# Routing each tile of tokens while the output projection runs, in a decoder layer with 32 experts

## The chip, the cores and the metric

The kernel runs on one core of one Trainium2 chip. The metric is the device time of one execution in microseconds (us). Engines are named as in the profile: PE (TensorE), with PEld for its weight loads, DVE (VectorE), ACT (ScalarE), POOL (GpSimd) and SP (SyncE, which here only issues DMAs).

## What is computed

The reference is one layer on 1,024 tokens plus 16 meta tokens, width 1,024:

```
h = concat(meta_tokens, x)                       # 1040 x 1024
y = mlstm_mixer(h, ...)                          # chunked linear attention, ends with out @ w_out
h = layer_norm(ALPHA * h + y, ln1_g, ln1_b)
grp_logits = h @ w_group + b_group               # 4 groups
g_top = argmax(grp_logits)
exp_logits = (h @ w_router + b_router)           # 4 groups x 8 experts
top_vals, top_idx = top_k(exp_logits of group g_top, 2)
weights = softmax(grp_logits)[g_top] * softmax(top_vals)
for each expert e, on its tokens:  y += weight * (silu(x @ w_gate[e]) * (x @ w_up[e])) @ w_down[e]
h = layer_norm(ALPHA * h + y, ln2_g, ln2_b)
```

Each expert's gate, up and down matrices are 1,024 x 512, 1,024 x 512 and 512 x 1,024 numbers. Blocks of up to 128 tokens of one expert are called items here. There is one item for each of the 32 experts, and up to 16 more where an expert has over 128 tokens.

## The kernel before

All engines run their own instruction streams and meet at semaphores; the order on each engine is written out by hand. Large matrices are multiplied as three products: a tensor is split into a high part (`whi`, `xhi`, made by ACT) and a low part (`wlo`, `xlo`, the rest, made by DVE), and PE adds high x high, high x low and low x high (`mm3`, L1332 to L1334).

The stages are: input projections; eight chunks of attention (`scores`, `values`, `keys`, `attend`); the output projection, tile by tile (128 tokens each); the routing; the experts; the second layer norm.

**Output projection.** `out_half(i, q)` computes half of tile i's rows on PE (24 products of 128x512). On DVE `residual(i, q)` adds the scaled residual into `z1`, and `row_norm(i)` makes the normalised rows: `bn_stats` and `bn_aggr` for mean and variance, a subtraction and a product with `g1` (L1057), `rsqrt_column` (ten small operations), and a last pass (L1061) into `h1t`. POOL stores `h1t` to memory (`h1_rows`). PE transposes it (`h1_T`, L1555), ACT copies the transpose to `h1T`, and PE computes the 36 logits of the tile (`logits`, L1563); DVE adds the bias (L1066) into `lg`. On PE the order is `out_half(i, 0)`, `logits(i - 2)`, `out_half(i, 1)`, `h1_T(i - 1)`.

**Routing.** When the logits of all eight tiles are there, DVE works on all tiles at once: the best group, the best two of its eight experts, one-hot rows (`r_oh`), and their running sum over the tiles (`r_acum`). PE turns these into each token's rank in its expert's list (L1602 to L1604). DVE turns ranks into an item number and a slot, for the lists past 128 tokens as well (`r_kn`, `r_eq`, `r_ohr`, L1226), and PE adds up the token lists with 32 products (L1608). From them DVE makes `tokrow` (which row of `h1_rows` each slot of each item takes) and `dstrow`, and signals `routed`. SP, ACT and POOL wait for `routed`.

**Experts.** POOL copies the item's column of `tokrow` into `tix` and gathers the rows into `xg` with an indirect DMA (L537). PE transposes them (`rows_T`, L1619), ACT and DVE split them (`xg_hi`, `xg_lo`), and PE runs gate, up and down. `lo_expert(j, k, p)` on DVE (L1104) makes the low part of half p of matrix k of item j; `times_up` (L1262) multiplies the activated gate with up, `hidden_T` (L1649) transposes the product, and `hidden_lo` (L1266) splits it. The order on PE in `item(j)` is `up(j)`, first part of the gate of j+1, `hidden_T(j)`, the rest of that gate, `rows_T(j + 2)`, `down(j)`. Items 0 and 1 stand ahead of a loop, the last two behind it. SP loads a half matrix as soon as `lo_expert` has released its buffer.

Of the kernel before, what the change touches and what calls it, by code (L numbers as in the profile page):

```python
# [12 lines left out]
P = 128  # L13
# [32 lines left out]
COLS = (4, 5, 0, 1, 2, 3)  # L46

# [18 lines left out]
def build(nc, hcat, w_in, b_gates, head_norm_w, w_out, ln1_g, ln1_b, w_group, b_group, w_router,  # L66
# [7 lines left out]
    ys = nc.dram_tensor("expert_rows", (2 * T, D), F32).ap()  # L74

# [47 lines left out]
    lmv = at("lmv", [P, 4])  # L123
    lg = at("lg", [P, NT, GROUPS + NE])
# [49 lines left out]
    wgr = at("wgr", [P, KC, GROUPS + NE])  # L174
    bgr = at("bgr", [P, GROUPS + NE])
# [7 lines left out]
    ks = at("ks", [P, H, P])  # L183

# [25 lines left out]

    cursor[0] = route_base
    KN = 2 * NT
    r_iota = at("r_iota", [P, P])
    r_eq4 = at("r_eq4", [P, NT, GROUPS])
    r_oh4 = at("r_oh4", [P, NT, GROUPS])
    r_g4 = at("r_g4", [P, NT, GROUPS])
    r_prod = at("r_prod", [P, NT, GROUPS, PER_GROUP])
    r_in = at("r_in", [P, NT, PER_GROUP])
    r_t8 = at("r_t8", [P, NT, PER_GROUP])
    r_oh8 = at("r_oh8", [P, 2, NT, PER_GROUP])  # L220
    r_s = at("r_s", [P, 16, NT])
    r_kn = at("r_kn", [P, 10, KN])
    r_oh = at("r_oh", [P, KN, NE])
    r_pr = at("r_pr", [P, KN, NE])
    r_rk = at("r_rk", [P, NT, NE])
    r_cnt = at("r_cnt", [P, NE])
    r_ex8 = at("r_ex8", [P, NE, 8])
    r_ex = at("r_ex", [P, 4, NE])
    r_c8 = at("r_c8", [P, KN, 8])
    r_thr = at("r_thr", [P, 8])  # L230
    r_a = at("r_a", [P, NT + 1, NE], BF16)
    r_acum = at("r_acum", [P, NT + 1, NE], BF16)
    r_ohr = at("r_ohr", [P, KN, P], BF16)
    r_eq = at("r_eq", [P, KN, ITEMS], BF16)
    r_rhs = at("r_rhs", [P, 2, KN, ITEMS], BF16)
    r_val = at("r_val", [P, 2, KN])
    r_v = at("r_v", [P, 2, ITEMS])
    r_e = at("r_e", [1, 3, ITEMS])
    r_cmp = at("r_cmp", [1, EXTRA, NE])
    assert cursor[0] <= route_base + 2 * PIECE * 4  # L240
# [12 lines left out]
    Z_BANK = (0, 1, 4, 5)  # L253

    S = {}

    def sem(name):
# [24 lines left out]
        gtok_mm g_neg g_exp g_one g_ln g_lf b_mm g_a aT_mm m_rows mb_mm g_arg gate_exp  # L282
# [3 lines left out]
        r_exp r_arg r_hot r_item rk_mm r_rhs_done v2_mm routed pool_passed  # L286
# [34 lines left out]
    def _(sp):  # L321
# [71 lines left out]
        sp.dma_start(wgr[:, :, GROUPS:], w_router.rearrange("(p k) n -> p k n", k=KC)).then_inc(N["ln1_in"], 16)  # L393
        sp.dma_start(bgr[:, 0:GROUPS], vec(b_group, P)).then_inc(N["ln1_in"], 16)
        sp.dma_start(bgr[:, GROUPS:], vec(b_router, P)).then_inc(N["ln1_in"], 16)
# [5 lines left out]
        sp.dma_start(b1[:], vec(ln1_b, P)).then_inc(N["ln1_in"], 16)  # L401
        for c in range(2, NT):
            load_qk(c)
            load_o(c)
        sp.wait_ge(N["v_mm"], len(VU))
# [12 lines left out]
        sp.wait_ge(N["routed"], 1)  # L418
# [36 lines left out]
    def _(pool):  # L455
# [20 lines left out]
        g.memset(ones[:], 1.0).then_inc(N["consts"], 1)  # L476

# [16 lines left out]
        pool.wait_ge(N["lo_done"], lo_count(4))  # L494
        for b in range(2):
            last = g.memset(vext[b][:, :, DV:DV + 1], 1.0)
        last.then_inc(N["ones_ready"], 1)

        for i in range(NT):
            pool.wait_ge(N["h1_done"], i + 1)  # L500
            pool.dma_start(h1_dram[i * P:(i + 1) * P, :], h1t[i % 2][:]).then_inc(h1_stored[i % 2], 16)

        pool.wait_ge(N["y_mm"], 2 * NT)
        g.iota(r_iota[:].bitcast(I32), [[1, P]], base=0, channel_multiplier=0)
        g.iota(r_thr[:].bitcast(I32), [[P, 8]], base=P, channel_multiplier=0)
# [45 lines left out]
        for j in range(4):  # L551
            gather(j, j % 2)
# [1166 lines left out]
```

## Time and profile before

| | us |
|---|---|
| median of 3 runs (lowest, highest) | 1224.57 (1224.02, 1225.34) |
| the profiled execution | 1223.59 |
| its span in the profile | 1221.4 |
| PE busy | 1074.9 (88%) |
| DVE busy | 796.3 (65%) |
| ACT busy | 615.6 (50%) |

The span is what the profiler covers; what lies around it took 2.2 us in the profiled execution. A line of a timeline gives the start, the duration, engine, line, operation, output<-input by the names of the program, shape, count, and in square brackets how long the engine was idle before and which instruction ended that. The granted clock (PEclk) is a share of 2.4 GHz: 1.00 is 2.4 GHz and 0.50 is 1.2 GHz.

### The profile page before, as it was taken

To read this page: it belongs to the slowest core of one execution; us is meant where nothing else is said; L and a number is where in the kernel's file an instruction comes from. 1 tells how busy PE (TensorE), PEld (TensorE's weight loads), DVE (VectorE), ACT (ScalarE), POOL (GpSimd) and SP (SyncE) were. 2 spreads that over 40 slices of the span, in tenths; PEclk is the share of its full clock that TensorE was granted. 3 is DMA by queue.
4 is the path that set the end of the run, shared out by engine and by line. 5 is a ranking of instruction groups with operands and counts; after the bars stand their busy time and mean duration, and the time that the engine had idled before them with its cause. 6 is when DMAs were issued, how large, how long until landed. Compare 5 with 4: busy or idle time off the path is not lost.

```text
span 1221.4 us, 15159 instructions
## 1 busy us (share of the span) xinstructions
PE 1074.9 (88%) x5217; PEld 890.4 (73%) x5217; DVE 796.3 (65%) x1038; ACT 615.6 (50%) x655; POOL 219.5 (18%) x207
## 2 busy tenths in 40 slices
PE   6999999999999899813799999999999999999700
PEld 5878899588887688713688888888888888888500
DVE  3310421234646675563798889899888989988378
ACT  4311221123335210110878888887888888788511
POOL 2001111000000000013033323323332332232100
PEclk9999999999999899955899999999999999999955
DMA  7513314302013222332799999999999999998672
GB/s 247 186 70 121 112 44 124 108 18 69 36 69 104 104 87 86 115 144 87 278 366 360 387 389 382 389 404 378 377 388 380 376 384 394 387 384 314 244 305 103
DMA packets 62616, 284.00 MB, mean 233 GB/s; under 512 B 13896, under 2 KB 13896, under 8 KB 36976
## 3 DMA queue, kind: packets, MB, share of 16 engines
q1 hardware_dynamic: 49584, 254.09, 54.8%
q0 software_dynamic: 12992, 29.38, 6.5%
q8 instruction: 24, 0.39, 0.1%
q14 instruction: 16, 0.13, 0.0%
HBM read 266.61 MB, written 33.55 MB: 246 GB/s over the span
## 4 chain that ended last, share of the span: by engine, by line
PE 85%; DVE 7%; DMA 3%; issue 2%; DVEq 1%; ACT 1%; POOL 0%; SPq 0%; POOLq 0%
PE bank L1332 25%; PE bank L1333 24%; PE bank L1334 24%; PE bank L1619 2%; PE bank L1649 1%; PE bank L1514 1%; PE bank L1516 1%; PE bank L1519 1%; DMA raw_out<-l_w_out 1%; PE bank L1563 1%; DVE hh L1310 1%; DVE yy L1316 1%; DMA xt<-hcat 1%; DMA xg<-h_rows,tix 1%; PE bank L1476 1%
## 5 line engine op out<-in xcount | busy, mean ns | idle before, releaser
L1332 PE MATMUL bank<-whi,xghi 128*128 128x512 f32 x512 | 204.4, 399 | 2.8 <-DVE xglo L1257 1.4
L1334 PE MATMUL bank<-whi,xglo 128*128 128x512 f32 x512 | 201.1, 393 | 0.0
L1333 PE MATMUL bank<-wlo,xghi 128*128 128x512 f32 x512 | 200.7, 392 | 0.0
L1104 DVE TENSOR_TENSOR wlo<-raw_down,whi 128x2048 fp32r<-128x2048 f32 x64 | 146.5, 2292 | 37.0 <-ACT whi L727 37.0
L1332 PE MATMUL bank<-whi,xhi 128*128 128x512 f32 (+1 forms) x400 | 163.6, 409 | 2.7 <-ACT vext L664 1.6
L1333 PE MATMUL bank<-wlo,xhi 128*128 128x512 f32 (+1 forms) x400 | 159.2, 398 | 0.0
L1334 PE MATMUL bank<-whi,xlo 128*128 128x512 f32 (+1 forms) x400 | 158.5, 396 | 0.0
L1104 DVE TENSOR_TENSOR wlo<-raw,whi 128x2048 fp32r<-128x2048 f32 x64 | 146.3, 2288 | 8.2 <-ACT whi L727 7.2
L1104 DVE TENSOR_TENSOR wlo<-raw_up,whi 128x2048 fp32r<-128x2048 f32 x64 | 146.2, 2285 | 0.0
L727 ACT ACTIVATE whi<-raw_up 128x2048 fp32r<-128x2048 f32 x64 | 122.3, 1914 | 24.7 <-PE bank L1334 24.7
L727 ACT ACTIVATE whi<-raw_down 128x2048 fp32r<-128x2048 f32 x64 | 122.3, 1912 | 23.7 <-PE bank L1334 23.7
L547 POOL DMA_INDIRECT expert_rows<-yt,dix x32 | 58.6, 1830 | 380.9 <-ACT yt L750 380.9
L727 ACT ACTIVATE whi<-raw 128x2048 fp32r<-128x2048 f32 x64 | 122.2, 1913 | 2.5 <-PE bank L1334 0.9
L1332 PEld LDWEIGHTS bank<-whi,xghi 128*128 128x128 f32 x512 | 97.5, 190 | 22.8 <-DVE xglo L1257 1.8
L1334 PEld LDWEIGHTS bank<-whi,xglo 128*128 128x128 f32 x512 | 97.0, 189 | 20.9
L1333 PEld LDWEIGHTS bank<-wlo,xghi 128*128 128x128 f32 x512 | 97.3, 190 | 19.2
L1332 PE MATMUL bank<-whi,ghi 128*128 128x512 f32 x256 | 102.2, 399 | 1.4 <-DVE glo L1266 1.4
L1334 PE MATMUL bank<-whi,glo 128*128 128x512 f32 x256 | 100.2, 391 | 0.0
L1333 PE MATMUL bank<-wlo,ghi 128*128 128x512 f32 x256 | 100.1, 391 | 0.0
L1332 PEld LDWEIGHTS bank<-whi,xhi 128*128 128x128 f32 (+1 forms) x400 | 75.0, 188 | 22.2 <-issue 3.1
L1334 PEld LDWEIGHTS bank<-whi,xlo 128*128 128x128 f32 (+1 forms) x400 | 74.6, 187 | 19.6
L1333 PEld LDWEIGHTS bank<-wlo,xhi 128*128 128x128 f32 (+1 forms) x400 | 74.8, 187 | 16.4
(298 smaller groups left out, 1590.8 us busy)
## 6 DMA issues: line engine op xcount, KB each, us to landing
raw<-l_w_gate SPq DMA_DIRECT2D x64, 1024.0 KB, 7.8
raw_up<-l_w_up SPq DMA_DIRECT2D x64, 1024.0 KB, 7.9
raw_down<-l_w_down SPq DMA_DIRECT2D x64, 1024.0 KB, 8.3
raw<-l_w_in SPq DMA_DIRECT2D x5, 2048.0 KB, 9.8
yy<-expert_rows SPq DMA_DIRECT2D x8, 1024.0 KB, 12.2
xt<-hcat SPq DMA_DIRECT2D x8, 512.0 KB, 3.3
o_rows<-stage POOLq DMA_DIRECT2D x16, 256.0 KB, 2.6
qkT<-qk_rows SPq DMA_DIRECT2D x16, 256.0 KB, 3.5
```

Of the source, the lines that this page charges most:

```text
L547: g.indirect_dma_start(ys[0:2 * T, :], bass.IndirectOffsetOnAxis(dix[b][:].bitcast(U32), 0), yt[b][:], None, bounds_check=last_row, oob_is ...
L727: a.activation(whi[k][:, halves(p)], raw_e[k][:, halves(p)], ACT.Copy).then_inc(e_hi[k], 1)
L1104: tt(wlo[k][:, halves(p)], raw_e[k][:, halves(p)], whi[k][:, halves(p)].bitcast(F32), ALU.subtract).then_inc(e_lo[k], 1)
L1310: stt(hh[n], yy[n][:, 1, :], wts[:, n, 1:2], hh[n], ALU.mult, ALU.add, accum_out=fsum[:, n:n + 1])
L1316: stt(yy[n][:, 1, :], hh[n], fneg[:, n:n + 1], g2, ALU.add, ALU.mult)
L1332: t.matmul(out, lh, rh, start=first, stop=False)
L1333: t.matmul(out, lh, rl, start=False, stop=False)
L1334: return t.matmul(out, ll, rh, start=False, stop=last)
L1476: last = t.matmul(ps[F_BANK[1]][:, h * P:(h + 1) * P], qkT[b][:, 1, h, :], qkT[b][:, 0, h, :], start=True, stop=True)
L1514: t.matmul(ps[N_BANK[h % 2]][:, 0:DV + 1], ew[:, h, :], vext[c % 2][:, h, :], start=True, stop=False)
L1516: t.matmul(ps[N_BANK[h % 2]][:, 0:DV + 1], qsT[:, h, :], cst[:, h, :], start=False, stop=True).then_inc(N["n_mm"], 1)
L1619: last = t.transpose(ps[q][:, k * P:(k + 1) * P], xv[:, 4 * q + k, :], ident[:])
```

## The change

Routing is taken apart into a piece for each tile that runs during the output projection.

- The logits are computed from the rows before normalisation. With z the row, m its mean, r the reciprocal deviation, the logits are r * (z @ (g W) - m * (g @ W)) + b @ W + bias. So W is scaled by `ln1_g` on ACT once, the two rows g @ W and b @ W (`logit_constants`, 8 products on PE in the attention of chunk 2) go through memory to all partitions (`cgb`), and PE transposes `z1` (`z_T`) where it transposed `h1t`. The 4 group logits are padded to 8 columns.
- `top_two(i)` on DVE picks the group and the two experts of one tile with `max` and `max_index`, which give the eight largest values and their places. `ranks(i)` on PE and `slots(i)` on DVE give the rank in the list, and `token_list(i)` adds the tile's part to the lists in one PSUM bank, which collects over all eight tiles. Only slots 0 to 127 of each expert are handled there.
- `item_count` (how many items there are) comes after `routed` and has a semaphore of its own, `routed_n`. The lists past 128 tokens (`past_128`, `list_past_128`, `rows_past_128`) are made inside items 0 and 1, the expert weights (`expert_weights`, with two exponentials on ACT) in the last item.
- The rows are normalised and stored by `h1_rows(i)`, later than before in DVE's order; ACT issues the store (`h1_store`), where POOL did.
- The constants (`r_iota` and others) are made by POOL at the start of the kernel. The clearing of `xg` is gone, and the first six gathers take their index from `tokrow` with no copy.

`past_128` is 11 DVE operations, the last a one-hot of 128x2048 as `r_ohr` was (L1226); `list_past_128` is 32 products of 128x16 on PE.

The old routing of all tiles at once (L1127 to L1250, some 70 DVE operations) goes; it is not shown. The core of the diff ("..." marks what is left out):

```diff
 @block.scalar
+        def logit_constants():
+            act.wait_ge(N["cc_mm"], 1)
+            a.activation(ccs[:], ps[N_BANK[0]][0:2, CC_COLS], ACT.Copy).then_inc(N["cc_cp"], 1)
+            for k in range(KC):
+                last = a.activation(wgr[:, k, :], wgr[:, k, :], ACT.Copy, scale=gbc[:, k, 0:1])
+            last.then_inc(N["wg_scaled"], 1)
+            act.wait_ge(N["cc_cp"], 1)
+            act.dma_start(cc_dram, ccs[:]).then_inc(N["cc_out"], 16)
...
         for i in range(NT - 1):
-            h1_T(i)
+            z_T(i)
+            h1_store(i)
         act.wait_ge(N["y_mm"], 2 * NT - 1)
         for p in range(2):
             hi_expert(0, 0, p)
-        h1_T(NT - 1)
...
+        z_T(NT - 1)
+        h1_store(NT - 1)
         for p in range(2):
             hi_expert(0, 1, p)
-        act.wait_ge(N["routed"], 1)
...
 @block.vector
+        def stats(i):
...
+            rsqrt_column(lmv[:, b, 2:3], lmv[:, b, 1:2], lmv[:, b, 3:4])
+        def h1_rows(i):
...
+            stt(h1t[b][:], z1[b][:], lmv[:, b, 0:1], g1[:], ALU.subtract, ALU.mult)
+            dve.drain()
+            stt(h1t[b][:], h1t[b][:], lmv[:, b, 2:3], b1[:], ALU.mult, ALU.add).then_inc(N["h1_done"], 1)
...
+        def top_two(i):
+            b, row = i % 2, lg[:, i, :]
+            dve.wait_ge(N["lg_mm"], i + 1)
+            stt(row, cgb[:, 0, :], lmv[:, b, 0:1], ps[F_BANK[0]][:, 0:NL], ALU.mult, ALU.add).then_inc(N["lg_done"], 1)
+            dve.drain()
+            stt(row, row, lmv[:, b, 2:3], cgb[:, 1, :], ALU.mult, ALU.add)
+            dve.drain()
+            v.max(r_gv[:, i, :], row[:, 0:GPAD])
+            dve.drain()
+            v.max_index(r_gi[:, i, :], r_gv[:, i, :], row[:, 0:GPAD])
+            dve.drain()
+            tt(r_pen[:], iota_g, r_gi[:, i, 0:1].to_broadcast([P, GROUPS]), ALU.not_equal)
+            dve.drain()
+            stt(r_in[:].rearrange("p (g e) -> p g e", g=GROUPS), r_pen[:].unsqueeze(2).to_broadcast([P, GROUPS, PER_GROUP]), NEG,
+                row[:, GPAD:].rearrange("p (g e) -> p g e", g=GROUPS), ALU.mult, ALU.add)
+            dve.drain()
+            v.max(r_tv[:, i, :], r_in[:])
+            dve.drain()
+            v.max_index(r_ti[:, i, :], r_tv[:, i, :], r_in[:])
+            dve.drain()
+            tt(r_oh[:, i], iota_e, r_ti[:, i, 0:2].unsqueeze(2).to_broadcast([P, 2, NE]), ALU.is_equal)
+            dve.drain()
+            tt(r_a[:, i, :], r_oh[:, i, 0, :], r_oh[:, i, 1, :], ALU.add).then_inc(N["r_hot"], 1)
+            wait(dve, N["list_mm"], i - 1)
+            tt(r_rhs[b][:, 0], r_oh[:, i], r_val0[:].unsqueeze(2).to_broadcast([P, 2, NE]), ALU.mult)
+            ts(r_rhs[b][:, 1], r_oh[:, i], float(2 * P * i), None, ALU.mult)
+            dve.drain()
+            tt(r_acum[:, i + 1, :], r_acum[:, i, :], r_a[:, i, :], ALU.add)
+        def slots(i):
+            dve.wait_ge(N["rk_mm"], i + 1)
+            dve.drain()
+            for k in range(2):
+                stt(r_junk[:, k, :], r_oh[:, i, k, :], 1.0, ps[F_BANK[0]][:, RANK_COLS], ALU.mult, ALU.mult, accum_out=r_rank[:, i, k:k + 1])
+            dve.drain()
+            tt(r_ohr[i % 2][:], iota_s, r_rank[:, i, :].unsqueeze(2).to_broadcast([P, 2, P]), ALU.is_equal).then_inc(N["r_slot"], 1)
...
+        for i in range(3, NT):
             residual(i, 0)
-            if i > 1:
-                logits(i - 2)
+            top_two(i - 1)
+            h1_rows(i - 1)
+            slots(i - 1)
             residual(i, 1)
-            row_norm(i)
+            stats(i)
+        top_two(NT - 1)
...
+        h1_rows(NT - 1)
+        slots(NT - 1)
+        dve.wait_ge(N["list_mm"], NT)
+        token_rows(F_BANK[1], LIST_COLS, 0).then_inc(N["routed"], 1)
         for p in range(2):
             lo_expert(0, 0, p)
...
+        item_count()
+        xg_lo(0, 0)
         for p in range(2):
             lo_expert(0, 1, p)
-        xg_lo(0, 0)
         xg_lo(1, 1)
...
         def item(j, b, ahead=2):
...
             hidden_lo(j)
+            if not ahead:
+                expert_weights()
+            if isinstance(j, int) and j == 1:
+                rows_past_128()
...
                 lo_expert(j + 1, 2, 0)
                 lo_expert(j + 1, 2, 1)
+            if isinstance(j, int) and j == 0:
+                past_128()
 @block.tensor
         out_half(1, 0)
         out_half(1, 1)
         gated_T(NT - 1)
-        out_half(2, 0)
-        h1_T(0)
-        out_half(2, 1)
+        out_half(2, 0, range(0, 2))
+        z_T(0)
+        out_half(2, 0, range(2, KC))
         logits(0)
-        h1_T(1)
+        z_T(1)
+        out_half(2, 1, range(0, 4))
+        ranks(0)
+        out_half(2, 1, range(4, KC))
+        token_list(0)
+        logits(1)
         for i in range(3, NT):
-            out_half(i, 0)
-            logits(i - 2)
-            out_half(i, 1)
-            h1_T(i - 1)
-        logits(NT - 2)
-        h1_T(NT - 1)
+            out_half(i, 0, range(0, 2))
+            z_T(i - 1)
+            if i == 3:
+                ranks(1)
+            out_half(i, 0, range(2, KC))
+            if i == 3:
+                token_list(1)
+            logits(i - 1)
+            out_half(i, 1, range(0, 4))
+            ranks(i - 1)
+            out_half(i, 1, range(4, KC))
+            token_list(i - 1)
+        z_T(NT - 1)
         logits(NT - 1)
+        ranks(NT - 1)
+        token_list(NT - 1)
...
         def item(j, b, ahead=2):
...
             hidden_T(j)
+            if isinstance(j, int) and j == 1:
+                list_past_128()
```

## Rows read from the trace of the kernel before

**Rows 1.** The page: busy time, share and instructions of each engine.

```profile
PE 1074.9 (88%) x5217; PEld 890.4 (73%) x5217; DVE 796.3 (65%) x1038; ACT 615.6 (50%) x655; POOL 219.5 (18%) x207
```

**Rows 2.** Waits: engine, line, releaser: us in total, times, longest us.

```profile
PE bank L1602 <- DVE r_acum L1172: 14.9, 1, 14.9
PE bank L1608 <- DVE r_rhs L1228: 12.3, 1, 12.3
PE bank L1649 <- DVE gu L1262: 5.7, 2, 4.8
...
DVE hh L1307 <- DMA yy<-expert_rows: 16.6, 2, 15.4
```

**Rows 3.** The chain that ended last, in order of time: start, us, what.

```profile
483.92 0.89 PE bank L1555 x8
...
504.19 1.71 PE bank L1563 x16
...
559.28 9.30 DMA xg<-h_rows,tix
...
572.07 0.79 PE bank L1332
```

**Rows 4.** Timeline of DVE in the output projection.

```profile
483.96 0.69 DVE L1044 SCALAR_TENSOR_TENSOR z<-hres,bank 128x512 f32<-128x512 f32 x1 [5.44 <-PE bank L1334]
484.74 1.29 DVE L1050 BATCH_NORM_STATS2 lst<-z 128x6 f32<-128x512 f32 x2
...
486.39 1.29 DVE L1057 SCALAR_TENSOR_TENSOR z<-z,lmv,g 128x1024 f32<-128x1024 f32 x1
...
490.02 1.29 DVE L1061 SCALAR_TENSOR_TENSOR h1t<-z,lmv,b 128x1024 f32<-128x1024 f32 x1
...
497.76 0.69 DVE L1044 SCALAR_TENSOR_TENSOR z<-hres,bank 128x512 f32<-128x512 f32 x1 [5.44 <-PE bank L1334]
...
511.57 0.69 DVE L1044 SCALAR_TENSOR_TENSOR z<-hres,bank 128x512 f32<-128x512 f32 x1 [5.12 <-PE bank L1334]
```

**Rows 5.** Timeline of DVE in the routing.

```profile
531.65 0.19 DVE L1136 TENSOR_TENSOR r_oh<-r_iota,r_s 128x32 f32<-128x32 f32 x1
531.91 0.43 DVE L1139 TENSOR_TENSOR r_prod<-lg,r_oh 128x256 f32<-128x256 f32 x1
532.41 0.29 DVE L1142 TENSOR_TENSOR r_prod<-r_prod 128x128 f32<-128x128 f32 x1
...
548.62 2.28 DVE L1226 TENSOR_TENSOR r_ohr<-r_iota,r_kn 128x2048 bf16<-128x2048 f32 x1
```

**Rows 6.** Timeline of ACT behind the output projection.

```profile
512.01 1.09 ACT L717 ACTIVATE h1T<-bank 128x512 f32<-128x512 f32 x2 [12.72 <-PE bank L1555]
512.99 3.71 ACT L727 ACTIVATE whi<-raw 128x2048 fp32r<-128x2048 f32 x2
```

**Rows 7.** DMA issues by line: KB each, median us to landing.

```profile
h_rows<-h1t POOLq DMA_DIRECT2D x8, 512.0 KB, 2.9
```

**Rows 8.** The gathered rows' tile, all 32 gathers.

```profile
DMA to landing us min/median/max: 4.1/9.0/10.4
```

**Rows 9.** Timeline of SP around the first gather.

```profile
558.50 2.53 SPq L382 DMA_DIRECT2D raw_up<-l_w_up  x2
```

**Rows 10.** Windows: busy us (instructions) by engine, PEclk, DMA share, GB/s.

```profile
592.00:593.00 1.00, 0.00 (x0) 0.00 (x0) 1.00 (x1) 1.00 (x1) 0.00 (x0) 0.87 0.95 336
...
599.00:600.00 1.00, 1.00 (x4) 0.74 (x4) 1.00 (x2) 0.00 (x0) 0.00 (x0) 0.72 1.05 442
```

**Rows 11.** Timeline of PE, the transposes in items 0 and 1.

```profile
594.35 1.13 PE L1649 MATMUL bank<-ident,gu 128*128 128x128 f32 x4 [4.83 <-DVE gu L1262]
614.56 0.63 PE L1649 MATMUL bank<-ident,gu 128*128 128x128 f32 x4
```

**Rows 12.** Timeline of DVE in item 1.

```profile
607.92 4.58 DVE L1104 TENSOR_TENSOR wlo<-raw_down,whi 128x2048 fp32r<-128x2048 f32 x2 [1.07 <-ACT whi L727]
612.78 0.69 DVE L1262 TENSOR_TENSOR gu<-sg,bank 128x512 f32<-128x512 f32 x1 [0.28 <-PE bank L1334]
```

More of the change, by code:

```diff
@@ new lines, in build @@
+    r_in = at("r_in", [P, NE])
+    r_ex = at("r_ex", [P, 3, NE])
+    assert cursor[0] <= offsets["hnw"]
+    r_rhsx = [over("r_oh", f"r_rhsx{i}", [P, 2, NT, 2, EXTRA], BF16)[:, i] for i in range(2)]
+    cursor[0] = offsets["qsT"]
+    r_ohr = [at(f"r_ohr{i}", [P, 2, P], BF16) for i in range(2)]
+    r_rhs = [at(f"r_rhs{i}", [P, 2, 2, NE], BF16) for i in range(2)]
+    r_junk = at("r_junk", [P, 2, NE])
+    r_t1 = at("r_t1", [P, NE])
+    r_big = at("r_big", [P, NE])
+    r_g4 = at("r_g4", [P, NT, GROUPS])
@@ L548, in scatter @@
                                  bounds_check=last_row, oob_is_err=False).then_inc(scattered[b], 16)
+        pool.wait_ge(N["routed"], 1)
+        for s in range(2):
+            pool.wait_ge(h1_stored[s], 16 * (NT // 2))
         for j in range(4):
@@ L704, in _ @@
                 gated_hi(c - 1)
+            if c == 2:
+                logit_constants()
             if c < NT - 1:
@@ L709, in _, with h1_store, z_T @@
         gated_hi(NT - 1)
-        def h1_T(i):
+        def h1_store(i):
+            act.wait_ge(N["h1_done"], i + 1)
+            act.dma_start(h1_dram[i * P:(i + 1) * P, :], h1t[i % 2][:]).then_inc(h1_stored[i % 2], 16)
+        def z_T(i):
             for q in range(2):
@@ L1091, in _ @@
         gate_rows(NT - 1)
-        row_norm(0)
+        stats(0)
         gated_lo(NT - 1)
-        for i in range(1, NT):
+        logit_terms()
+        residual(1, 0)
+        h1_rows(0)
+        residual(1, 1)
+        stats(1)
+        residual(2, 0)
+        top_two(0)
+        h1_rows(1)
+        slots(0)
+        residual(2, 1)
+        top_two(1)
+        stats(2)
+        slots(1)
+        for i in range(3, NT):
             residual(i, 0)
-            if i > 1:
-                logits(i - 2)
+            top_two(i - 1)
+            h1_rows(i - 1)
+            slots(i - 1)
             residual(i, 1)
-            row_norm(i)
-        logits(NT - 2)
+            stats(i)
+        top_two(NT - 1)
         def lo_expert(j, k, p):
@@ L1415, in maxima, with logit_constants @@
             last.then_inc(N["mb_mm"], 1)
+        def logit_constants():
+            pe.wait_ge(N["ln1_in"], 16 * 8)
+            pe.wait_ge(N["ones_ready"], 1)
+            pe.wait_ge(N["num_done"], 8)
+            for k in range(KC):
+                last = t.matmul(ps[N_BANK[0]][0:2, CC_COLS], gbc[:, k, :], wgr[:, k, :], start=k == 0, stop=k == KC - 1)
+            last.then_inc(N["cc_mm"], 1)
         pe.wait_ge(N["consts"], 1)
```

449 lines of the change are left out of this document (214 added, 235 removed).

## The prediction

> **What bounds the kernel now.** I read the page first: PE is busy for 88% of the span [rows 1], so a change pays where PE stands still, and costs wherever it makes PE wait. The list of waits comes next. PE waits 14.9 us for the running sum of one-hot rows and 12.3 us for the last list operand [rows 2]. Both belong to one stretch, which the chain in order of time and DVE's timeline show: the last product of the output projection ends at about 511.4 (DVE's residual starts at 511.57), the first gather is issued at 559.28, and the first expert product starts at 572.07 [rows 3, 4]. From 511.4 to 572.07, 60.7 us, PE does almost nothing, and the chain runs through DVE and one DMA. The change works on the first 47.9 us of it.
>
> The output projection ahead of it is bound by PE. DVE's residual starts at 483.96 and at 497.76 and waited 5.44 us for PE each time [rows 4]: a tile takes 13.80 us. Eight transposes take 0.89 and the logits 1.71 [rows 3], which leaves 11.20 for 48 products, 0.233 each. DVE's idle 5.44 us per tile are the only room for routing.
>
> **The per-tile pieces on DVE.** Two consecutive starts are the price of one step with its wait: 0.26 us for 32 elements (531.65 to 531.91) and 0.50 for 256 (531.91 to 532.41) [rows 5]. `top_two` up to `r_hot` is ten steps. Eight plain ones make 2.1 with the PSUM operand. The trace has no `max` or `max_index`. Bounds: `max_index` costs at least one plain step, 0.26, which makes 2.6 for the chain with small extras for pointer scalars; at most, eight separate passes over 32 elements, so one step of 256, 0.50 for each of the two `max` and the two `max_index`, and the chain is 3.75. I take 0.43 for `max_index` and 0.26 for `max`, nearer to the plain step because the rows are short: **2.95**. The rest of `top_two` is three steps, 0.60. `h1_rows` is two passes of 1.28 or 1.29 [rows 4], 2.65 with waits. `slots` is two steps of 32 and one of 256, 1.05. 
>
> **What that does to PE.** I count from the end of `out_half(i, 0)`, from tile 4 on. Logits ready +1.83; `r_hot` +4.78; end of `top_two` +5.38; `h1_rows` +8.03; `slots` +9.08. PE arrives at `ranks(i - 1)` at +4.5 and waits 0.3; it arrives at `token_list(i - 1)` at +7.9 and waits until +9.15, another 1.2. Then 0.3 for the list, 1.4 for six products, 0.95 for `z_T`, 4.2 for 18 products: the next round begins at **+16.0, not +13.8**. What queues behind these waits on PE is the output projection itself. Worked out in the same way, tiles 2 and 3 wait more, 8.1 us in all: `z_T(0)` comes earlier than `h1_T(0)` did and stands behind DVE's low part of the last attention rows (1.6), and `stats` stands in front of the first pieces. Tiles 4 to 7 wait 5.0. More PE work ahead of the last half tile: one more `z_T` and logits (2.6), seven `ranks` and six lists at 0.3 (3.9). Sum 8.1 + 5.0 + 6.5: the projection ends **19.5 us later**, at 530.8. The bounds of `top_two` give 17.0 and 25.
>
> The waits rest on a count of steps. The Trainium skill, VectorE: DVE Perf Modes, section on the TRN2 errata, says that each instruction pays a fixed latency, and that many small tiles pay it per tile. The trace agrees: 8 times the elements cost 0.50 against 0.26 [rows 5]. By this rule the per-tile form speaks against the change, since eight tiles pay 17 steps each for what one batch did in some 70.
>
> **The tail.** From 530.8: `residual(7, 1)` waits for `slots(6)` and ends at 532.6, `z_T(7)` at 533.7. ACT comes out of the store of tile 6 at 531.5 and must do the expert halves first, 3.7 [rows 6]; the copies (1.1) end at 536.3. The logits take between 1.71 and twice that, as the clock may fall in this pause; I take 2.5: 538.9. Then DVE: 2.95 + 0.6 + 2.65 make 545.2, `slots` 546.2, list 0.5, `token_rows` 0.85: `routed` at 547.6. POOL also waits for the store of tile 7, issued at 545.2 and landed after 2.9 [rows 7], 548.2; so this store is late last, not the lists. The gather goes out at **548.4**, 17.6 us after the projection where it was 47.9: **-30.3**.
>
> **The gather.** It took 9.3 us with two half matrices issued at 558.50 in front of it [rows 3, 9]; the quickest of 32 took 4.1 [rows 8]. Now `lo_expert(0, 0, 0)` ends at 549.9, and the halves that it releases are issued behind the gather. I take 7.0, between the two: **-2.3** (0 to -5.2). The 3.5 us from landing to the first product stay; DVE is out of `item_count` (about 4 us) at 556, in time.
>
> **Added work behind it.** `logit_constants` on PE: eight products like the logits, **+1.7** (0.8 to 3: ACT then has nine short operations and a DMA ahead of its copy of the values). `past_128` on DVE: the one-hot 2.28 [rows 5], two of 512 at 0.7, three of 256 at 0.43, two of 128 at 0.27, three short ones 0.6: 6.1 us. It stands straight in front of `times_up(1)`, which before waited 0.28 for PE after DVE's last low part (607.92 + 4.58) [rows 12]. So gate times up is ready at 619.3, and `hidden_T(1)`, which ran at 614.56 [rows 11], waits 4.8. In the equal pause of item 0 (4.83) the clock fell to 1.2 GHz in 592 to 593 and came back in 599 to 600, 5.2 us after PE resumed at 594.35 [rows 10, 11]; half of that, 2.5, is lost. `list_past_128`: 32 short products, 0.9. Sum **+8.2**. `expert_weights` costs DVE nothing, since DVE waits 15.4 us for the last rows [rows 2]; its exponentials delay ACT's last copies a little, **+0.4** (0 to 2).
>
> At nothing: the constants on POOL's queue at the start (it then waits for the first store anyway), SP's four small loads, ACT's issue of the stores. The cover is idle queue time; without it each costs under 1 us. `item_count` delays nothing, for `lo_expert(1, 0, 0)` waits for the activated gate.
>
> **Sum.** 19.5 - 30.3 - 2.3 + 1.7 + 8.2 + 0.4 = -2.8. The profiled execution has a span of 1221.4 and took 1223.59; it would be 1218.6 and 1220.8. It lies 1.0 under the median 1224.57, so the median is **1221.7**.
>
> **Rivals.**
> 1. *DVE's routing chain is longer than I count.* Each 0.1 us more in `top_two` comes eight times, seven tiles on PE and once in the tail: 0.8. At the upper bound, 3.75, this is +6.4: **1228**. It decides from 0.36 us per tile on. For it: four operations without a row, on a chain that is already what PE waits for. Against it: short rows, and all other short steps here cost the same. Chance 0.27.
> 2. *The clock falls in the projection too.* PE pauses 1.2 us per tile and in tiles 2 and 3 up to 1.7. If five of these cost 2.5 us like the one in item 0: **1234**. Against it: in item 0 the clock held for 3 us of pause before it fell [rows 10]. Chance 0.06.
> 3. *`past_128` is hidden*, because other work on DVE leaves room or PE's gate begins later: without stall and clock loss, -7.3: **1214**. Against it: the slack before `times_up(1)` was 0.28. Chance 0.15.
> 4. *The projection keeps its pace* (13.8 plus 0.6 a tile), and the change saves all that the waits promise: 13.1 less, **1209**. It needs DVE's chain shorter by some 1.5 us per tile. Chance 0.07.
>
> The forecast itself holds 0.45, with a range of its own of 1217 to 1226.
>
> **Numbers.** About 0.2% (2.4 us) can be told from no change in this kernel: under 1222.1 is faster, over 1227.0 slower. The forecast's case gives 0.24 faster, 0.14 same, 0.07 slower; rivals 3 and 4 give 0.22 faster; rival 1 0.05 same and 0.22 slower; rival 2 0.06 slower. So faster 0.46, same 0.19, slower 0.35. The range reaches from rival 3, with the gather at its quickest, 1212, to rival 2, 1234.
>
> **What would show it.** In the profile after: 16 us between residuals in the projection, PE waiting for DVE's `r_ohr` or `r_a` there; the last `out_half` ending near 532 (with `logit_constants` counted); the gather near 550, and the first expert product near 561; PE waiting 4.8 us for `gu` in item 1 and a second dip of the clock behind it. The forecast is wrong if `max_index` takes over 0.6 us, if the waits in the projection are small, or if the wait in item 1 is missing.

## The result and the profile after

The changed kernel takes 1217.31 us (median of 4 runs, 1216.20 to 1217.95), the kernel before, run beside it, 1224.95 us (4 runs, 1224.02 to 1225.77). The ratio is 0.9937, with a 95% interval of 0.9920 to 0.9954: 7.6 us or 0.6% faster. The profiled execution took 1216.2 us, with a span of 1213.5 where it was 1221.4.

The page gives the busy time of each engine, as in [rows 1]:

```profile
PE 1080.5 (89%) x5279; PEld 891.8 (73%) x5279; DVE 809.8 (67%) x1152; ACT 618.9 (51%) x665; POOL 206.5 (17%) x192
```

PE is busy 5.6 us longer than before, in a span that is 7.9 us shorter: it stands still less. The list of waits shows where:

```profile
PE bank L1731 <- DVE gu L1297: 10.0, 3, 4.8
PE bank L1629 <- DVE r_ohr L1150: 9.7, 8, 3.7
PE bank L1701 <- DMA xg<-h_rows,tokrow: 9.4, 1, 9.4
...
PE bank L1622 <- DVE r_a L1137: 4.7, 3, 2.9
PE bank L1615 <- ACT h1T L751: 2.5, 1, 2.5
PE bank L1607 <- DVE xlo L1066: 1.6, 1, 1.6
```

The two long waits of [rows 2], 14.9 and 12.3 us, are gone. In their place stand eight for `r_ohr`, 0.84 to 0.95 us each in the projection and 3.70 at the last tile, and three for `r_a`. The wait for `gu`, two times before, now comes three times. PE's timeline, with the wait ahead of each instruction in brackets:

```profile
497.57 0.26 PE L1629 MATMUL bank<-r_rhs,r_ohr 128*128 128x32 bf16 x4 [0.85 <-DVE r_ohr L1150]
512.99 0.27 PE L1629 MATMUL bank<-r_rhs,r_ohr 128*128 128x32 bf16 x4 [0.84 <-DVE r_ohr L1150]
528.40 0.27 PE L1629 MATMUL bank<-r_rhs,r_ohr 128*128 128x32 bf16 x4 [0.84 <-DVE r_ohr L1150]
529.00 1.16 PE L1607 MATMUL bank<-ident,z 128*128 128x128 f32 x8 [0.33 <-DVE z L1080]
532.65 3.64 PE L1615 MATMUL bank<-wgr,h1T 128*128 128x40 f32 x16 [2.50 <-ACT h1T L751]
539.23 0.21 PE L1622 MATMUL bank<-r_a,beforeb 128*128 128x32 bf16 x1 [2.94 <-DVE r_a L1137]
543.17 0.29 PE L1629 MATMUL bank<-r_rhs,r_ohr 128*128 128x32 bf16 x4 [3.70 <-DVE r_ohr L1150]
...
552.87 1.95 PE L1701 MATMUL bank<-ident,xg 128*128 128x128 f32 x8 [9.39 <-DMA xg<-h_rows,tokrow]
...
579.24 1.13 PE L1731 MATMUL bank<-ident,gu 128*128 128x128 f32 x4 [4.79 <-DVE gu L1297]
...
604.29 1.13 PE L1731 MATMUL bank<-ident,gu 128*128 128x128 f32 x4 [4.32 <-DVE gu L1297]
```

From one `r_ohr` to that of the next tile is 15.4 us, and each time PE waits 0.84 or 0.85 for it; behind the last product all waits are DVE's, ACT's and the gather's. The last line is the new stall in item 1, where PE waited for nothing in [rows 11]. Following the same points through both traces (starts in us; the forecast in the last column is the prediction's own sum) gives:

| point | before | after | shift | forecast |
|---|---|---|---|---|
| last product of the projection | 511.13 | 527.17 | +16.0 | +21.2 |
| first gather issued | 559.28 | 545.81 | -13.5 | -9.1 |
| first expert product | 572.07 | 556.23 | -15.8 | -11.4 |
| transposes of `gu` in item 0 | 594.35 | 579.24 | -15.1 | |
| transposes of `gu` in item 1 | 614.56 | 604.29 | -10.3 | |
| end of the span | 1221.4 | 1213.5 | -7.9 | -2.8 |

So 15.8 us are won up to the first expert product, and 7.9 are given back: 5.5 of it by the transposes of item 1, the rest by `gu` of item 2 (DVE starts it at 623.04, where it was 630.48: -7.4).

### The profile page after: what moved, and what is told of

Read it like the earlier page. It is cut to its first block, busy times and chain, and to the rows that moved or that the text cites. A ratio compares the mean times of both kernels' runs of the same rounds, so it can differ in the third digit from the quotient of the medians.

```text
span 1213.5 us, 15480 instructions
## 1 busy us (share of the span) xinstructions
PE 1080.5 (89%) x5279; PEld 891.8 (73%) x5279; DVE 809.8 (67%) x1152; ACT 618.9 (51%) x665; POOL 206.5 (17%) x192
## 4 chain that ended last, share of the span: by engine, by line
PE 81%; DVE 10%; DVEq 3%; DMA 2%; issue 2%; ACT 1%; SPq 0%; ACTq 0%; POOLq 0%
PE bank L1374 23%; PE bank L1376 23%; PE bank L1375 23%; PE bank L1701 2%; PE bank L1731 1%; PE bank L1615 1%; PE bank L1566 1%; PE bank L1568 1%; DVE wlo L1278 1%; PE bank L1571 1%; DMA xt<-hcat 1%; DVE h1t L1097 1%; DVE hh L1352 1%; DVE yy L1358 1%; DVEq L1096 1%
## 5 line engine op out<-in xcount | busy, mean ns | idle before, releaser
L1278 DVE TENSOR_TENSOR wlo<-raw,whi 128x2048 fp32r<-128x2048 f32 x64 | 146.4, 2289 | 10.3 <-ACT whi L761 9.0
L761 ACT ACTIVATE whi<-raw 128x2048 fp32r<-128x2048 f32 x64 | 122.4, 1915 | 15.8 <-PE bank L1376 14.1
L1375 PEld LDWEIGHTS bank<-wlo,xghi 128*128 128x128 f32 x512 | 97.8, 191 | 19.6
```

What stands on the lines that cost most here:

```text
L761: a.activation(whi[k][:, halves(p)], raw_e[k][:, halves(p)], ACT.Copy).then_inc(e_hi[k], 1)
L1278: tt(wlo[k][:, halves(p)], raw_e[k][:, halves(p)], whi[k][:, halves(p)].bitcast(F32), ALU.subtract).then_inc(e_lo[k], 1)
L1375: t.matmul(out, lh, rl, start=False, stop=False)
```

## Experiments

All kernels ran beside the kernel before, and ratios are to that. Differences in us are between medians. The kernel before had a median of 1224.95 us beside the changed kernel, 1225.18 beside experiments 1, 2 and 4, 1224.58 beside 3, 5, `h1_first` and `combined`, and 1223.49 beside `store_clear`, `count_first`, `combined_swap` and `best`; so a difference across these groups holds up to 1.7 us that no edit made, and there the ratios are the better guide. The runs also differ by some 3 us in where they stand when the projection's tail begins (`z_T(0)` starts between 430.4 and 433.7 in the profiles), so stretches are compared from starts inside one trace.

### 1. Top-8 operations done twice

```diff
 def top_two(i):
...
-    v.max(r_gv[:, i, :], row[:, 0:GPAD])
-    dve.drain()
-    v.max_index(r_gi[:, i, :], r_gv[:, i, :], row[:, 0:GPAD])
-    dve.drain()
+    for _ in range(2):
+        v.max(r_gv[:, i, :], row[:, 0:GPAD])
+        dve.drain()
+        v.max_index(r_gi[:, i, :], r_gv[:, i, :], row[:, 0:GPAD])
+        dve.drain()
...
```

The pair for `r_tv` and `r_ti` is doubled in the same way.

```diff
+    for _ in range(2):
+        v.max(r_tv[:, i, :], r_in[:])
+        dve.drain()
+        v.max_index(r_ti[:, i, :], r_tv[:, i, :], r_in[:])
+        dve.drain()
```

> Each pair of max and max_index in top_two is done twice, with the same results. By the starts in the changed kernel's timeline a pair is 0.56 and 0.60 us, so top_two is 1.16 us longer. Theory (the serial chain on DVE paces PE in seven tiles and the tail): 8 x 1.16 = 9.3 us more, 1226.6, period 16.6 us. Rival (PE's order absorbs part of it, since ranks waited for nothing from tile 3 on): less than 5 us more. A third outcome, the longer pauses lower the clock in the projection: over 13 us more.

Measured: 1226.38 us (1.0014, 1.0004 to 1.0025), 9.1 more than the changed kernel. The list of waits of this kernel:

```profile
PE bank L1624 <- DVE r_a L1139: 15.1, 8, 4.1
PE bank L1631 <- DVE r_ohr L1152: 9.2, 7, 3.7
```

The 0.5 us less for `r_ohr` and 10.4 more for `r_a` are what was added: PE now waits at `ranks` of every tile. DVE's residual starts at 503.71 and at 520.29, a period of 16.58 for 15.42 in the same order of the changed kernel. This is the prediction's slope, 0.8 us of time for each 0.1 us in `top_two`, found at 0.78. The granted clock stayed at 1.00 from 470 to 536; before that, behind a wait of 2.68 us at the first `ranks`, it was at 0.50 or on its way there or back from 444 to 448.

### 2. `slots` before `h1_rows`

```diff
 for i in range(3, NT):
     residual(i, 0)
     top_two(i - 1)
-    h1_rows(i - 1)
     slots(i - 1)
+    h1_rows(i - 1)
```

> In the loop of the projection (tiles 2 to 6) slots(i - 1) stands before h1_rows(i - 1) on DVE instead of behind it. Theory (the projection is slow because PE waits at each token list for r_ohr, behind the 2.65 us of h1_rows): the waits of 0.84 us at L1629 vanish, the period goes from 15.4 to 14.5 us, the time falls by 4.5 us to 1212.8. Rival (DVE's total work per tile sets the period, not the order): the wait moves to z_T or ranks, the period stays at 15.4, within 1 us of the changed kernel.

Measured: 1213.17 us (0.9906, 0.9887 to 0.9924), 4.1 less. Its list of waits:

```profile
PE bank L1629 <- DVE r_ohr L1150: 4.8, 3, 3.7
PE bank L1607 <- DVE xlo L1066: 1.6, 1, 1.6
PE bank L1607 <- DVE z L1080: 1.3, 1, 1.3
```

Five of the eight waits are gone, the period is 14.53 (residuals at 495.15 and 509.68), and DVE still waits 1.5 us per tile for PE. DVE's work per tile is the same, so these 0.9 us per tile came from its order: `r_ohr`, for which PE waits, stood behind the two passes of `h1_rows`. What remains over 13.80 is 0.7 a tile, in which PE waits for nothing from tile 4 on; `ranks` and the lists are what it has to do there beyond before.

### 3. The kernel before, with only the constants moved

```diff
 def _(pool):
...
+    g.iota(r_iota[:].bitcast(I32), [[1, P]], base=0, channel_multiplier=0)
...
+    g.tensor_copy(r_val[:, 1, :], r_val[:, 1, :].bitcast(I32)).then_inc(N["r_arg"], 1)
     for u in range(UNITS):
         store(u)
...
-    pool.wait_ge(N["y_mm"], 2 * NT)
-    g.iota(r_iota[:].bitcast(I32), [[1, P]], base=0, channel_multiplier=0)
...
-    g.tensor_copy(r_val[:, 1, :], r_kn[:, 1, :].bitcast(I32)).then_inc(N["r_arg"], 1)
```

> The kernel before, with only this of the change: POOL makes r_iota, r_thr and the token values at the start, in tiles of their own, instead of behind the projection. DVE waited 5.00 us for them at 530.48. Theory (those 5 us were on the path to the first gather): 5 us below the kernel before, 1219.9, so that over half of the measured 7.6 us could be had without routing by tiles. Rival (POOL's part runs beside, and something else, such as the last stores or the list operands, takes its place): under 1.5 us.

Measured: 1219.12 us (0.9950, 0.9935 to 0.9965), 5.5 less than the kernel before. In the timeline of the kernel before, POOL stood 9.28 us between making its integers and casting them, without a cause named by the profile, and DVE waited for it:

```profile
529.56 0.29 POOL L511 CAST r_iota<-r_iota 128x128 f32<-128x128 int32 x1 [9.28 <-issue]
...
530.48 0.19 DVE L1120 TENSOR_REDUCE r_s<-lg 128x8 f32<-128x32 f32 x1 [5.00 <-POOL r_val L515]
```

What POOL waited for at this drain is not shown. Its store of tile 7 was issued at 519.21 and took 8.4 us to land, to 527.6, so it was under way for most of that time. Without the wait the first reduction follows the last logits at once (524.30 and 524.60) and the token rows come 4.9 us sooner against the residuals. So 5.5 of the 7.6 us could be had with the routing left in one batch. Routing by tiles has them too, since it makes these constants at the start; over this kernel its own net gain is 1.8 us between medians. That is not clear of noise: the intervals of the two ratios, 0.9920 to 0.9954 and 0.9935 to 0.9965, overlap.

### 4. `past_128` moved, and left out

```diff
     for p in range(2):
         lo_expert(0, 1, p)
+    past_128()
     xg_lo(1, 1)
...
-        if isinstance(j, int) and j == 0:
-            past_128()
```

> past_128 moves on DVE from the end of item 0 to between lo_expert(0, 1) and xg_lo(1, 1), where DVE stood idle for 4.9 us. Theory (its 5.9 us stood in front of times_up(1), so that PE waited 4.3 us in item 1, the clock fell, and 8.4 us were given back): PE's second wait for gu is under 0.5 us, the dip of the clock in item 1 is gone, and the time is 7.5 us below the changed kernel, 1209.8. Rival (the 8.4 us come from list_past_128's 32 products or from the gathers' transfers, and DVE's block is not their cause): within 1.5 us of the changed kernel, 1216 to 1218, the wait for gu still there.

> Leaves out the lists of tokens past 128 per expert altogether: past_128 and its token rows on DVE, the 32 products on PE, and POOL's wait for them. Theory (DVE's block costs about 7.5 us, the 32 products 0.9): 8.4 us below the changed kernel, 1208.9, and 0.9 below the kernel with past_128 moved. Rival (part of what was given back behind the first gather is something else, such as transfers): the gap is under 6 us.

The second kernel has no `past_128`, no `list_past_128` and no `rows_past_128`, so it handles no token past the 128th of an expert. Measured: moved 1210.71 us (0.9882, 0.9864 to 0.9900), 6.6 less; left out 1209.10 us (0.9873, 0.9853 to 0.9893), 8.2 less. In the changed kernel DVE's timeline in item 1 reads:

```profile
593.18 4.58 DVE L1278 TENSOR_TENSOR wlo<-raw_down,whi 128x2048 fp32r<-128x2048 f32 x2 [1.07 <-ACT whi L761]
597.67 0.28 DVE L1191 TENSOR_TENSOR r_c<-r_rank,r_thr 128x128 f32<-128x128 f32 x1
...
601.35 2.29 DVE L1207 TENSOR_TENSOR r_ohrx<-r_iota,r_kn 128x2048 bf16<-128x2048 f32 x1
603.55 0.68 DVE L1297 TENSOR_TENSOR gu<-sg,bank 128x512 f32<-128x512 f32 x1
```

The `gu` of [rows 12] used to follow the low parts; now 5.9 us stand between them. And PE's timeline of the kernel with `past_128` moved:

```profile
582.11 1.13 PE L1730 MATMUL bank<-ident,gu 128*128 128x128 f32 x4 [4.79 <-DVE gu L1297]
...
602.74 0.63 PE L1730 MATMUL bank<-ident,gu 128*128 128x128 f32 x4
603.21 0.96 PE L1638 MATMUL bank<-r_rhsx,r_ohrx 128*128 128x16 bf16 x32
```

The pause in item 1 is gone and the transposes take 0.63 again, as in [rows 11], not 1.13. From the first expert product to `gu` of item 2 it is 66.8 us in the changed kernel, 60.4 with the block moved and 58.4 without it; the kernel before has 58.4. So what was given back is the handling of the lists past 128: 6.4 us by the place of `past_128`, 2.0 by the 32 products and what else remains. The rival (the gathers' transfers) is out.

### 5. ACT's copies first

```diff
+z_T(NT - 1)
 for p in range(2):
     hi_expert(0, 0, p)
-z_T(NT - 1)
 h1_store(NT - 1)
```

> ACT copies h1T of tile 7 before it does the two halves of whi (3.7 us). Theory (those halves stood in front of the copies, as the prediction says, so logits(7) came late and at half the clock): copies start near 529.9 instead of 531.5, PE's pause before logits(7) shrinks from 2.50 to about 0.7 us, top_two(7) starts as stats(7) ends, 3.3 us sooner, and the time falls by 3 us to 1214.3. Rival (the halves are needed as early as they are, so lo_expert(0, 0) and the first product move later by as much): within 1 us.

Measured: 1212.19 us (0.9899, 0.9884 to 0.9914), 5.1 less. PE's pause shrank to 0.78 as expected, and `top_two(7)` began 1.7 us sooner against the last residual, not 3.3, because the logits kept to half the clock (414 ns for each of 16, in both kernels) in spite of the shorter pause. The profiles give 1.7 us up to the first product and 1.2 by item 2, besides a `z_T(0)` that lay 0.9 earlier from causes ahead of the edit. What the 1.2 us behind the first product are is open; the direction and most of the expected 3 us are shown, the 5.1 of the medians (4.7 by the ratios) is more than the profiles account for.

### 6. The last tile: the store and the gather

```diff
+h1_rows(NT - 1)
 top_two(NT - 1)
...
-h1_rows(NT - 1)
 slots(NT - 1)
```

> For the last tile h1_rows(7) stands before top_two(7) on DVE, in the 3.36 us in which DVE waited for logits(7). Theory (from the last product to the gather DVE's own sequence is the path): routed comes 2.65 us sooner and the store of tile 7, which was last, is early; the gather goes out about 3.8 us sooner, near 542, and the time falls by 3.6 us to 1213.7. Rival (the first gather is held by something else, or the gain is lost to a colder clock or to SP's halves in front of the gather): under 1.5 us.

Measured: 1216.37 us (0.9929, 0.9917 to 0.9941), only 0.9 less: the expectation failed. The token rows were 2.4 us sooner (541.62 for 544.03), but the first product was 1.5 us later. Two lines of its timeline (POOL, SP), and one of its DMA issues between 530 and 560 (the last number is the us to landing), show why:

```profile
544.00 3.16 POOL L551 DMA_INDIRECT xg<-h_rows,tokrow  x1 [329.83 <-DMA h_rows<-h1t]
...
544.03 2.53 SPq L404 DMA_DIRECT2D raw<-l_w_gate  x2
```

```profile
h_rows<-h1t ACTq DMA_DIRECT2D x1, 512.0 KB, 6.8
```

The store of tile 7, issued at 536.24, fell among the loads of `raw_up` and `raw_down` and landed only at 543.0; and the gather left together with the halves of gate(1). The windows of 541 to 542 us, of h1_first and then of the changed kernel, show it: the DMA engines (second number from the end) are full in the first and idle in the second, just ahead of its own store at 542.24.

```profile
541.00:542.00 1.00, 0.08 (x4) 0.00 (x0) 0.76 (x4) 0.00 (x0) 0.00 (x0) 0.50 1.01 418
541.00:542.00 1.00, 0.00 (x0) 0.00 (x0) 1.00 (x1) 0.00 (x0) 0.00 (x0) 0.50 0.00 0
```

Two kernels took these apart, both with `h1_first` in them:

```diff
 # store_clear, SP
+sp.wait_ge(N["h1_done"], NT)
 load_expert(0, 0, 2)
 # count_first, DVE
+item_count()
 for p in range(2):
     lo_expert(0, 0, p)
-item_count()
```

> h1_first, and SP waits until h1_rows(7) has been made before it issues the halves of raw_down(0). In h1_first the store of tile 7 was issued 6.0 us sooner than in the changed kernel but took 6.8 us to land instead of 2.6, under the loads of raw_up and raw_down, and the gather went out 0.96 us behind its landing, 2.4 us behind the token rows. Theory (the store of tile 7 holds the gather, and the loads hold the store): the store lands in under 4.5 us, the gather goes out near 542.8 instead of 544.0, and the time is 1 to 2 us below h1_first. Rival (POOL needs 2 us from the token rows whatever the store does): the gather stays 2.4 us behind the token rows.

> h1_first, and item_count stands on DVE before lo_expert(0, 0) instead of behind it, so the half matrices of gate(1), which lo_expert releases, go out about 4 us later. In h1_first they were issued 0.03 us behind the gather, whose issue then took 3.16 us instead of 1.3 to 1.6, and PE got the rows 10.4 us behind the gather instead of 7.1. Theory (the collision with these loads costs the 3.3 us): PE gets the rows 5 to 7 us behind the gather, first product near 553.5, the time 3.5 to 4.5 us below h1_first, 1212.5. Rival (the gather is slow for another reason): 10 us and no gain.

Measured: store_clear 1216.21 us (0.9935, 0.9915 to 0.9955), no gain; count_first 1209.28 us (0.9869, 0.9845 to 0.9893), 7.1 less than h1_first, where 3.5 to 4.5 were expected. Its first product starts at 552.64 for 557.71, 5.1 sooner, and `gu` of item 2 is 6.4 sooner (617.74 for 624.12); where the last 1.3 of these arise is open. The wait on SP did not do what it was for: SP issued the loads at 536.37, in front of the store at 536.38, which again took 6.9 us. That run does not test the store against loads. It does show that the store holds the gather, together with the others (us; landing is issue plus the time to landing):

| kernel | store issued | lands | token rows | gather | gate(1) halves against the gather | gather to PE |
|---|---|---|---|---|---|---|
| changed | 542.24 | 544.8 | 544.03 | 545.81 | 0.63 behind | 7.06 |
| slots_first | 539.05 | 541.7 | 540.84 | 542.61 | 0.64 behind | 6.99 |
| act_swap | 539.63 | 542.5 | 541.42 | 543.45 | 0.37 behind | 6.82 |
| h1_first | 536.24 | 543.0 | 541.62 | 544.00 | 0.03 behind | 10.35 |
| store_clear | 536.38 | 543.3 | 541.73 | 544.21 | 0.08 ahead | 9.50 |
| count_first | 536.94 | 543.7 | 542.32 | 544.74 | 3.79 behind | 4.54 |

In all six the gather goes out 0.9 to 1.0 us behind the store's landing, and 1.8 to 2.5 behind the token rows. So the store was last. Issued 6.0 us sooner in h1_first than in the changed kernel, it landed only 1.8 sooner. That the loads slow it rests on which stores were slow; no run keeps all else and takes the loads away. The last column is the second effect: with the halves 3.8 us behind, PE has the rows in 4.5 us; 0.4 to 0.6 behind, in 7; at the same time, in about 10. Lines of count_first, to be held against those of h1_first:

```profile
544.74 1.09 POOL L551 DMA_INDIRECT xg<-h_rows,tokrow  x1 [329.46 <-DMA h_rows<-h1t]
...
548.53 2.53 SPq L404 DMA_DIRECT2D raw<-l_w_gate  x2
```

### 7. Together

combined is `past_early`, `slots_first` and `h1_first` in one; combined_swap adds `act_swap`; best adds the edits of `count_first` and `store_clear` to that.

> The changed kernel with past_128 moved early, slots before h1_rows in the loop, and h1_rows(7) before top_two(7). If the three gains are apart from each other, in stretches of their own: 7.5 + 4.5 + 3.6 = 15.6 us below the changed kernel, 1201.7, and 23 below the kernel before. Rival (they overlap or the gathers' transfers and the store of tile 7 become the limit): under 12 us.

> combined, and ACT copies h1T of tile 7 before the halves of whi. In combined the store of tile 7 took 7.4 us under the loads and landed at 540.4, 1.0 us before the gather, 1.1 us behind the token rows. Theory (the store holds the gather there): the swap, worth 3 to 5 us alone, gives under 1.5 us here, 1203.4 to 1205. Rival (DVE's chain still holds the gather): 3 us, 1202.

> All together: past_128 early, slots before h1_rows in the loop, h1_rows(7) before top_two(7), h1T copies before whi on ACT, item_count before lo_expert(0, 0), raw_down(0) behind h1_rows(7). Against combined: the gather goes out near 539.2 instead of 541.4 (store clear, logits sooner, less 2.2), PE gets the rows in 5 to 6 us instead of 6.9 (less 1.7). Sum 1204.9 - 3.9 = 1201.0. Rival (raw_down(0) or gate(1) now come too late for item 0 and PE waits there instead): not below 1204.

Measured: combined 1204.90 us (0.9836, 0.9820 to 0.9852), 12.4 less than the changed kernel. The sum of the expected gains was 15.6; the gains measured alone (6.6, 4.1 and 0.9) make 11.6, so they add, and what is missing is that of h1_first. combined_swap 1207.41 us (0.9856, 0.9833 to 0.9880), above both of the expected times; best 1201.11 us (0.9810, 0.9789 to 0.9831), 22.4 less than the kernel before. In combined, the store landed at 540.4 and the gather went out at 541.41. In combined_swap, which looks better by its edits, the token rows came 1.3 us sooner against the last residual, the store took 7.6 us, and SP issued gate(1) 1.2 us ahead of the gather, which took 9.05 us to PE: the collision of h1_first again, so this kernel is no faster than combined. best removes the collision. PE's timeline in it:

```profile
543.94 1.94 PE L1701 MATMUL bank<-ident,xg 128*128 128x128 f32 x8 [7.67 <-DMA xg<-h_rows,tokrow]
547.29 0.79 PE L1374 MATMUL bank<-whi,xghi 128*128 128x512 f32 x1 [1.41 <-DVE xglo L1293]
```

The gather left at 539.71, 2.9 us behind the token rows and 1.0 behind the landing of the store, which still took 6.9 us. PE had the rows 4.23 us later. The sum of 1201.0 came out partly by luck. The gather left 1.7 us sooner than in combined (expected 2.2), but `z_T(0)` already lay 1.2 earlier, so the clear store gave about 0.5; the collision removed was worth 2.6 (6.86 to 4.23) where I gave it 1.7. That makes 3.1, and the ratios give 3.2; the expected 3.9 was reached by the medians, of which this group's lie about 1 us lower.

## Why the prediction was right, step by step

The time (1221.7 for 1217.3, within 0.4%) and the sign were right, and the shape was: the projection slower, the tail much shorter, and a stall of its own in item 1. The median lies in the likeliest case's range, at its low end. The gain was 2.9 us by the forecast and 7.6 measured, and "faster" had a chance of only 0.46, so the sign was no firm forecast. By the prediction's own steps:

**The per-tile pieces: right, a little too dear.** DVE's timeline of one tile in the changed kernel:

```profile
506.16 0.26 DVE L1118 SCALAR_TENSOR_TENSOR lg<-cgb,lmv,bank 128x40 f32<-128x40 f32 x1 [0.93 <-PE bank L1615]
...
506.85 0.17 DVE L1122 MAX8 r_gv<-lg 128x8 f32<-128x8 f32 x1
507.09 0.09 DVE L1124 MATCH_VALUE_LOAD r_gi<-r_gv,lg 128x8 f32 x1
507.17 0.16 DVE L1124 FIND_INDEX8 r_gi<-r_gv,lg 128x8 uint32<-128x8 f32 x1
507.41 0.16 DVE L1126 TENSOR_TENSOR r_pen<-r_iota,r_gi 128x4 f32<-128x4 f32 x1
...
507.92 0.20 DVE L1131 MAX8 r_tv<-r_in 128x8 f32<-128x32 f32 x1
...
508.82 0.18 DVE L1137 TENSOR_TENSOR r_a<-r_oh 128x32 bf16<-128x32 bf16 x1
...
509.39 1.28 DVE L1095 SCALAR_TENSOR_TENSOR h1t<-z,lmv,g 128x1024 f32<-128x1024 f32 x1
510.74 1.28 DVE L1097 SCALAR_TENSOR_TENSOR h1t<-h1t,lmv,b 128x1024 f32<-128x1024 f32 x1
512.13 0.19 DVE L1148 SCALAR_TENSOR_TENSOR r_junk<-r_oh,bank 128x32 f32<-128x32 bf16 x1
...
512.85 0.68 DVE L1080 SCALAR_TENSOR_TENSOR z<-hres,bank 128x512 f32<-128x512 f32 x1
```

A `max` is 0.24 and 0.27 us from its start to the next (0.26 taken), a `max_index` 0.32 (0.43 taken). The chain from the first step to the end of `r_a` is 2.84 (2.95; rival 1 needed a longer one, and its upper bound of 3.75 is 3.6 when its own terms are added up), what follows it up to `h1_rows` 0.4 (0.60), `h1_rows` 2.7 with its waits (2.65), `slots` 0.7 to 0.9 (1.05).
**What that does to PE: right in kind, 3.6 us too high.** The period is 15.4, not 16.0. The waits at the token lists came (0.84, forecast 1.2); those at `ranks` did not from `ranks(2)` to `ranks(6)`. PE's waits up to the last product are 5.9 us in tiles 2 and 3 (forecast 8.1) and 2.5 in tiles 4 to 7 (5.0); the rest of the delay, 7.5, is 1.0 more than the 6.5 that I gave to PE's added work. Experiments 1 and 2 show the mechanism: the slope is that of the count, and the order of two pieces on DVE is worth 4.1 us. Rival 4 fell, as the pace was not kept. Rival 2 was right about the clock in other runs, but not about its price. In the changed kernel's profile the clock stayed at 1.00 through the projection; in all other kernels with routing by tiles except combined_swap it fell to 0.50 for up to 4 us in tile 2 or 3. In h1_first:

```profile
451.00:452.00 1.00, 1.00 (x4) 0.60 (x4) 0.71 (x5) 0.00 (x0) 0.00 (x0) 0.50 0.01 4
```

It cost nothing there: from DVE's residual of tile 2 at 440.12 to that of tile 3 at 466.78 it is 26.66 us, and 26.68 in the changed kernel (439.90 to 466.58). The slower products took the place of a wait for `r_ohr`.

**`logit_constants`: wrong, +0.1 instead of +1.7.** Its products took 0.73 us:

```profile
297.27 0.73 PE L1464 MATMUL bank<-wgr,gbc 128*2 128x40 f32 x16
```

PE waits 7.2 us for DVE in the last attention chunk behind it, where it waited 7.5 before, and resumes 0.7 us later than before (403.12 for 402.42). At its next wait, 0.56 for ACT's `num`, the two traces are 0.1 us apart (416.28 and 416.18). The prediction put this work on PE's path without looking for later waits in which it could vanish.

**The tail: right.** From the end of the last product (527.6) to the gather it was 18.2 us (17.6). ACT's expert halves stood in front of the copies, the logits ran at half the clock (3.64 us, where 2.5 was taken), and the store of tile 7 came last, as said. It took 2.6 us (forecast 2.9), issued when the loads had landed; in the kernel before, the store of this tile took 8.4 us among them, which the median of eight that I took did not show. Its landing and the gather lie 1.0 us apart where the forecast left 0.2.

**The gather: right.** 7.06 us to PE against the forecast 7.0, for the reason given: the halves follow it. That it came out to 0.1 us is luck, since 7.0 was only a value between 4.1 and 9.3. Experiment 6 adds that the distance matters, from 4.2 to 10.4 us.

**`past_128`: right.** The stall was 4.3 us (4.8), the second dip of the clock came, and 7.9 us were given back by the end (8.2 with the lists); left out, it gave 8.2. Windows of the changed kernel, with the granted clock third from the end:

```profile
578.00:579.00 1.00, 0.00 (x0) 0.00 (x0) 1.00 (x2) 0.65 (x1) 0.00 (x0) 0.71 0.82 320
...
602.00:603.00 1.00, 0.00 (x0) 0.00 (x0) 1.00 (x1) 0.00 (x0) 0.00 (x0) 0.66 0.94 361
609.00:610.00 1.00, 1.00 (x6) 0.81 (x5) 1.00 (x2) 0.75 (x1) 0.00 (x0) 0.93 0.97 410
```

It fell in 602 to 603, in PE's pause, and was back by 609 to 610, 5 us after PE resumed at 604.29, as in item 0 and in [rows 10]. Rival 3 (hidden) is out.

**`expert_weights`: +0.4 forecast, nothing seen.** The shift at the last items, -7.8, is that of the end, -7.9.

The step that was off is thus the projection's delay, with `logit_constants` counted in: 21.2 forecast, 16.0 measured. Of the difference, 1.6 is work that vanished in later waits. The other 3.6 is 4.7 of waits that did not come, less 1.0 of more work on PE (the forecast's terms, 8.1, 5.0 and 6.5, make 19.6, where it says 19.5): in tiles 4 to 7 from small steps on DVE that each were 0.1 to 0.2 us dear (`r_ohr` was ready 8.75 us after `out_half`, not 9.15), the 2.2 in tiles 2 and 3 were not taken apart further.

## What to carry to other kernels

Before batched work is broken up to overlap it, look for the one wait in the batch that can simply be removed: here constants made too late were 5.5 of 7.6 us, and what the rest of the change gave was not clear of noise until its pieces were put in a better order. In a loop that two engines pass back and forth, put first on the one engine what the other waits for next, and count small steps as often as they come. A deferred block needs a place where its engine is idle, not one where it is only late; and of a transfer that ends a serial chain, ask which loads leave beside it, since to issue it sooner can put it among them.

## What the runs showed that I had not expected

- The store of tile 7, 512 KB, took 2.6 to 2.9 us when it was issued at 539 to 544, behind the loads of the expert's weights, and 6.8 to 7.6 us when issued at 532 to 537 among these loads of 1,024 KB each (six kernels). In the kernel before, issued at 519.21 among loads, it took 8.4.
- A gather's rows reached PE 4.2 to 4.5 us after its issue with the halves of a weight issued over 3 us later, 6.8 to 7.8 with them 0.3 to 0.6 later, and 9.1 to 10.4 with them at the same time or up to 1.2 ahead. Its issue on POOL itself went from 1.1 to 3.2 us.
- The clock had fallen to half by the logits of the last tile although PE had paused only 0.85, 0.33 and 0.78 us since its last product of the projection (act_swap): between these pauses it did only four products of 32 columns and eight transposes.
- In the kernel before, POOL stood 9.28 us at a drain behind its last store and its integers. The store landed at 527.6, 2.0 us before POOL went on; whether the drain waited for it is not shown, and this stays open.
